# First down projection: eight of its 22 k tiles as seven products of block sums, and the position biases moved behind them

## The chip, the core and the metric

The kernel runs on one core of a Trainium2 chip, in one launch. Its time is the device time of the whole program in microseconds (us). TensorE (PE) multiplies, VectorE (DVE), ScalarE (ACT) and GpSimd (POOL) do the elementwise work, SyncE (SP) issues most DMAs. Each engine runs its own program in order and waits on semaphores where the program says so.

## The reference

Two transformer blocks follow each other on 256 tokens of 1024 features, all in float32. The first mixes tokens by forgetting attention and a gated delta rule, the second by neighbourhood attention and pooling; each ends in a feed-forward part. The change is in the feed-forward part of the first:

```python
hn = rmsnorm(h, norm_ffn[l])
up = causal_dwconv(jnp.einsum('bsd,df->bsf', hn, w_up[l]), ffn_conv_w[l])
u_gate, u_val = jnp.split(up, 2, axis=-1)
h = h + jnp.einsum('bsf,fd->bsd', jax.nn.silu(u_gate) * u_val, w_down[l])
```

`D_FF` is 2816, so the down projection multiplies a 256 x 2816 activation by a 2816 x 1024 weight: 22 k tiles of 128. The second block's feed-forward part has the same sizes, without the convolution. The biases are the second block's `rpb`, which neighbourhood attention adds to its scores.

## The kernel before

**Numbers.** Every float32 operand of a large product is split into a rounded part and a rest (`hi` and `lo`), and a product is three matmuls: hi x hi, lo x hi, hi x lo. The weights are split while the kernel runs.

**Steps.** All large products form one list of 258 steps (`HALVES`). A step is half a weight panel: 128 x 1024 numbers. SP loads panels into three raw buffers (`fetch`, L2590). For step n ACT rounds the raw half into `panel_hi` (`split`, L1238, copy at L1236), DVE subtracts to get `panel_lo` (`split`, L1740, L1754), PE multiplies (`gemm`, L710, matmuls at L652). Both have four buffers: ACT may write step n when PE has finished step n-4. In every engine's loop the pass for step n first splits step n+3 and then does what else is due at n, so that each elementwise job has a fixed place in its engine's queue, between two splits.

**The up projection** (steps 97 to 140): from its second pair of panels on, four steps make a gate and a value product of two feature tiles (a round, numbered j = 0 to 10). Per round DVE has four `panel_lo`, two `ffn_scaled` (bank times the row factor, L2097), two times four convolution taps (`ffn_taps`, L2109), one `ffn_silu` (L2115) and one `ffn_lo` (L2119, the lo half of the activation); POOL has one `ffn_mul` (L2517); ACT rounds the activation (`ffn_hi`, L1455).

**The first down projection** (steps 141 to 162): four banks, 2 x 512 columns by 2 x 128 tokens; `DOWN_ORDER` (L83) says which four k tiles and which columns each panel has. Each step is two k tiles by 512 columns for both token tiles, 12 matmuls of 512 columns. Beside it DVE adds the window mask to the position biases, one head in each of the passes 144 to 151 (`MASK_AT`, `mask_rpb`, L2122). The biases were loaded in the up projection, in the passes of `RPB_AT` (112, 116, 120, 124), the pooling bands and weights four and eight passes later.

**Its end.** `END["down", 0]` is 159 and `END["down", 1]` is 162. At such a step DVE adds the two banks of that column half to the residual `h` (`add_to_h`, L2029) and sums squares. PE, after the step that follows (160 and 163), waits for both adds of that half and transposes `h` (`turn_x`, L754, matmuls at L768) for the next products (`qk2`). POOL (`gained`, L2505), ACT and DVE multiply and sum further for the next norm.

**The second down projection** (steps 231 to 258) already does its first eight k tiles in seven products, by Winograd's form of Strassen's scheme: the activation is cut by k tiles and tokens, the weights by k tiles and column halves, `GROUPS` = 2 times. The four weight blocks of a group (128 x 1024 each) are loaded early (`block_raw`); each of the seven steps of a group splits a block or a sum of blocks, and DVE makes the four sums in place (`add_block`, L1731), each behind the split named in `ADDED_BEHIND`. Sums of the activation (`act2_sums` on POOL, L2526, then ACT's and DVE's halves, L1523 and L2199) are made for j = 0 to 3. Such a step has 6 matmuls of 512 columns. `GROUP_ORDER` puts a block step (named) and a plain step (None) in turn. The seven products go to seven banks, and DVE combines three of them with the others at the end (`block_sums`, L2055), before the last adds.

**Layout of time:** the DVE pass for step n is `split(n+3)` with its sum of blocks, then the adds and turns at an `END`, then `ffn_lo`, `ffn_silu`, `ffn_taps`, `ffn_scaled`, then a mask.

Of the kernel before, what the change touches and what calls it, by code (L numbers as in the profile page):

```python
# [17 lines left out]
F32 = mybir.dt.float32  # L18
# [52 lines left out]
for _name, _n in (("ident", P), ("upper", P), ("ones", 4), ("causal", P), ("decay_mask", P),  # L71
# [11 lines left out]
DOWN_ORDER = [(k, c) for k in range(0, KF - 6, HALF) for c in range(2)] + [(k, c) for c in range(2) for k in (16, 20)]  # L83
# [7 lines left out]
DOWN2_ORDER = [(8, 0), (8, 1), (12, 0), (12, 1), (16, 0), (20, 0), (16, 1), (20, 1)]  # L91
BLOCKS = ("b11", "b12", "b21", "b22")
GROUP_ORDER = [("b11", None, "b21", None, "b22", None, "t3", None, "t1", None, "t2", None, "t4", None),
               ("b11", None, "b21", None, "b22", None, "t3", None, "t1", "t2", None, "t4", None, None)]
ADDED_BEHIND = {"b11": "t1", "b21": "t3", "b22": "t2", "t3": "t4"}
BLOCK_BANK = {"b11": ("p1",), "b21": ("down2", 0, 0), "b22": ("down2", 1, 0), "t4": ("down2", 0, 1), "t1": ("p5",),
              "t2": ("p6",), "t3": ("p7",)}
SUM_3, SUM_1, SUM_2, SUM_4 = range(4)

# [5 lines left out]
def panels():  # L105
# [51 lines left out]
    for k, c in DOWN2_ORDER:  # L157
        add_wide(("down2", c), "act2", "w_down_2", k, min(HALF, KF - k), c * WIDE)
# [9 lines left out]
def with_blocks(halves):  # L168
    plain = [x for x in halves if PLAN[x[0]][0][0] != "down2"]
    down2 = iter(halves[len(plain):])  # L170
    return plain + [next(down2) if b is None else (None, g, b) for g, order in enumerate(GROUP_ORDER) for b in order] \
        + list(down2)
# [3 lines left out]
BLOCK_AT = {(g, b): n + 1 for n, (i, g, b) in enumerate(HALVES) if i is None}  # L176
# [5 lines left out]
          for i in range(len(PLAN))]  # L182
# [6 lines left out]
DOWN2_BANKS = [("down2", c, m) for c in range(2) for m in range(TT)] + [("p1",), ("p5",), ("p6",), ("p7",)]  # L189
TOUCHES = {key: [n + 1 for n, (i, _, b) in enumerate(HALVES)  # L190
                 if (BLOCK_BANK[b] == key if i is None else PLAN[i][0] == key[:2])] for key in DOWN2_BANKS}
for _c in range(2):
    END["down2", _c] = max(TOUCHES["down2", _c, m][-1] for m in range(TT))

# [20 lines left out]
BLOCKS_FROM = [END["up2", 1, 4], END["up2", 1, 6]]  # L215
# [6 lines left out]
RPB_AT = [END["up", 1, j] for j in (3, 4, 5, 6)]  # L222
MASK_AT = [END["up", 1, KF // 2 - 1] + 4 + i for i in range(HEADS)]
# [15 lines left out]
def build(nc, a, out, scratch_a, scratch_x, scratch_c):  # L239
    ctx = ExitStack()  # L240
    with ctx:
# [67 lines left out]
        gain_final = at("gain_final", [P, D], 19.5)  # L309
        sq2 = at("sq2", [P, TT, 2, PW], 23.5)  # L310
        block_at = [{"b11": 22, "b12": 22.5, "b21": 23, "b22": 23.5}, {"b11": 0, "b12": 0.5, "b21": 16.5, "b22": 21.5}]
        block_raw = [{b: at(f"block_{b}_{i}", [P, HALF * PW], block_at[i][b]) for b in BLOCKS} for i in range(2)]
        act_sums = [at(f"act_sums{i}", [P, 4, P], 21, skip=2048 * i) for i in range(2)]
        act_sums_hi = at("act_sums_hi", [P, 2 * GROUPS, 4, P], 18, F32R)
        act_sums_lo = at("act_sums_lo", [P, 2 * GROUPS, 4, P], 19.5, F32R)
# [188 lines left out]
        s_u_copied, s_block_sums = sem("p1_copied"), sem("block_sums")  # L504
# [45 lines left out]
        def down2_done(c, m):  # L550
            n = TOUCHES["down2", c, m][-1]
            return (s_half, n) if m or HALVES[n - 1][0] is None else filled(("down2", c, 0))
# [41 lines left out]
        def block_rows(g, b):  # L594
            r, c = int(b[1]) - 1, int(b[2]) - 1
            w = weights["w_down_2"][g * HALF * P:(g + 1) * HALF * P, wide(c)]
            return w.rearrange("(k r p) c -> r p k c", r=2, p=P)[r]
# [9 lines left out]
        def block_landed(g, b):  # L607
            return s_block[g][int(b[1]) - 1], 32

        def block_added(g, b):  # L610
            return s_block_add, len(ADDS) * g + ADDS.index(b) + 1
# [2152 lines left out]
```

## Time and profile before

| what | us |
|---|---|
| runs shown, median (lowest to highest) | 804.03 (802.47 to 804.63) |
| profiled execution, its own time | 802.98 |
| its span, first to last instruction | 801.5 |
| PE busy in the span | 795.6, 99% |
| DVE busy | 625.1, 78% |
| ACT busy | 457.2, 57% |
| POOL busy | 90.7, 11% |
| TensorE's granted clock | 1.000 of full speed throughout the span |

Some 1.5 us of the profiled execution lie outside its span. A timeline row gives the start, the busy time (of all its instructions, where it has several), the engine, the line, the operation, the tile written and the tiles read, their shapes and the count; in brackets the idle time ahead of it and what ended it. Two instructions of one engine may overlap by some 0.1 us, so the time from one start to the next is what an instruction costs its queue. Steps are counted along the `panel_lo` instructions of DVE, one a step.

### The profile page before, as it was taken

Reading aid. Unit: us, or ns where it says so; the run is one execution under the profiler, and the core shown is the slowest. Engines: PE = TensorE matmul, PEld = TensorE weight load, DVE = VectorE, ACT = ScalarE, POOL = GpSimd, SP = SyncE. Lnnn points to the kernel's source line nnn. Section 1 sums busy time; section 2 is a strip of 40 time slices with the busy share of each in tenths; the row PEclk is TensorE's granted clock in tenths of the full one; section 3 lists DMA queues with packets and bytes.
Section 4 is the critical chain, followed back from the end, with each engine's and each line's share of the span. In section 5 each row is a group of like instructions: output and inputs, shape, how many; then the busy total and the mean of one; then the engine's idle time right before and its main releaser. Section 6 shows DMA issues by size and latency. Waiting matters only on the chain. (4 is left out here: it accounts for less than half of the span.)

```text
span 801.5 us, 13178 instructions
## 1 busy us (share of the span) xinstructions
PE 795.6 (99%) x5164; PEld 696.8 (87%) x5164; DVE 625.1 (78%) x1035; ACT 457.2 (57%) x738; POOL 90.7 (11%) x77
## 2 busy tenths in 40 slices
PE   8999999999999999999999999999999999999998
PEld 6888888999898888899999998887778888888886
DVE  6888989785555766679999997486866898787977
ACT  6667677554535544456656563466665566555552
POOL 0001000010011302101101110011100333011100
PEclk9999999999999999999999999999999999999999
DMA  9654564557432555475687656464424666884331
GB/s 317 187 166 157 176 229 145 151 146 228 123 118 88 172 173 199 167 237 180 193 251 244 224 186 209 165 203 160 156 79 147 198 207 214 288 282 161 107 103 54
DMA packets 118125, 144.09 MB, mean 180 GB/s; under 512 B 11552, under 2 KB 86704, under 8 KB 117808
## 3 DMA queue, kind: packets, MB, share of 16 engines
q1 hardware_dynamic: 115616, 141.22, 54.7%
q10 hardware_dynamic: 2448, 2.03, 1.0%
q8 instruction: 41, 0.67, 0.3%
q14 instruction: 20, 0.16, 0.1%
HBM read 141.78 MB, written 1.46 MB: 179 GB/s over the span
## 5 line engine op out<-in xcount | busy, mean ns | idle before, releaser
L1754 DVE TENSOR_TENSOR panel_lo<-panel_raw,panel_hi 128x1024 fp32r<-128x1024 f32 x237 | 300.8, 1272 | 106.8 <-ACT panel_hi L1236 105.1
L652 PE MATMUL bank<-x_halves,panel_hi 128*128 128x256 f32 (+1 forms) x1536 | 367.0, 322 | 0.7 <-DVE x_halves L2222 0.7
L1236 ACT ACTIVATE panel_hi<-panel_raw 128x1024 fp32r<-128x1024 f32 (+1 forms) x239 | 252.2, 1057 | 152.9 <-PE bank L652 150.8
L652 PE MATMUL bank<-x_halves,panel_lo 128*128 128x256 f32 x1024 | 288.3, 282 | 0.0
L652 PEld LDWEIGHTS bank<-x_halves,panel_hi 128*128 128x128 f32 x1536 | 255.8, 190 | 23.3 <-issue 0.9
L652 PEld LDWEIGHTS bank<-x_halves,panel_lo 128*128 128x128 f32 x1024 | 195.0, 190 | 0.2
L652 PE MATMUL bank<-panel_hi,x_halves 128*128 128x512 f32 x384 | 122.1, 399 | 0.0
L652 PEld LDWEIGHTS bank<-panel_hi,x_halves 128*128 128x128 f32 x384 | 70.0, 188 | 14.4 <-DVE panel_lo L1754 0.6
L652 PE MATMUL bank<-panel_lo,x_halves 128*128 128x512 f32 x192 | 75.1, 391 | 0.0
L652 PE MATMUL bank<-panel_hi,act_hi 128*128 128x512 f32 x156 | 60.9, 390 | 0.2 <-DVE panel_lo L1754 0.2
L652 PE MATMUL bank<-panel_hi,act_lo 128*128 128x512 f32 x156 | 60.7, 389 | 0.0
L652 PE MATMUL bank<-panel_lo,act_hi 128*128 128x512 f32 x156 | 60.7, 389 | 0.0
L652 PEld LDWEIGHTS bank<-panel_lo,x_halves 128*128 128x128 f32 x192 | 36.0, 188 | 8.0
L2491 POOL TENSOR_TENSOR stats<-stats 128x2 f32<-128x2 f32 (+1 forms) x9 | 17.1, 1900 | 185.1 <-DVE stats L1768 104.0
L652 PEld LDWEIGHTS bank<-panel_hi,act_hi 128*128 128x128 f32 x156 | 29.3, 188 | 6.6 <-DVE panel_lo L1754 0.6
L652 PEld LDWEIGHTS bank<-panel_lo,act_hi 128*128 128x128 f32 x156 | 29.3, 188 | 6.1
L652 PEld LDWEIGHTS bank<-panel_hi,act_lo 128*128 128x128 f32 x156 | 29.3, 188 | 5.9
L1790 DVE SCALAR_TENSOR_TENSOR conv_acc<-conv_tmp,params,conv_acc 128x255 f32<-128x255 f32 (+2 forms) x72 | 30.5, 484 | 1.4 <-ACT conv_acc L1236 1.4
L2517 POOL TENSOR_TENSOR ff_tanh<-ff_tanh,ff_val 128x512 f32<-128x512 f32 x11 | 17.2, 1564 | 112.4 <-DVE ff_tanh L2115 112.4
L2496 POOL TENSOR_TENSOR key_bias<-key_bias,constants 128x128 f32<-128x128 f32 x16 | 8.9, 577 | 176.6 <-DMA key_bias<-gate_sums 176.6
L2524 POOL TENSOR_TENSOR f_tanh<-f_tanh,ff_val 128x512 f32<-128x512 f32 x11 | 15.2, 1385 | 94.0 <-DVE f_tanh L2191 94.0
L1748 DVE TENSOR_TENSOR panel_lo<-block_b,panel_hi 128x1024 fp32r<-128x1024 f32 x14 | 18.2, 1301 | 5.2 <-ACT panel_hi L1236 4.8
(312 smaller groups left out, 1017.1 us busy)
## 6 DMA issues: line engine op xcount, KB each, us to landing
panel_raw<-in_w_in SPq DMA_DIRECT2D x35, 1024.0 KB, 5.3
panel_raw<-in_w_up SPq DMA_DIRECT2D x30, 1024.0 KB, 5.4
panel_raw<-in_w_down SPq DMA_DIRECT2D x16, 1024.0 KB, 5.0
panel_raw<-in_w_gate SPq DMA_DIRECT2D x10, 1024.0 KB, 5.4
panel_raw<-in_w_out SPq DMA_DIRECT2D x8, 1024.0 KB, 5.0
panel_raw<-in_w_in SPq DMA_DIRECT2D x11, 512.0 KB, 4.7
panel_raw<-in_w_branch_fox SPq DMA_DIRECT2D x4, 1024.0 KB, 5.0
panel_raw<-in_w_branch_gdn SPq DMA_DIRECT2D x4, 1024.0 KB, 5.0
```

The source lines that it names most:

```text
L652: return e.matmul(o, l, r, start=start, stop=stop, skip_group_check=True)
L1236: return e.activation(o, i_, ACT.Copy, scale=scale)
L1748: e.tensor_tensor(wlo[w], block_raw[g][KEPT_IN[b]], whi[w].bitcast(F32), ALU.subtract) \
L1754: e.tensor_tensor(lo, raw_view(i, k0, kt), hi.bitcast(F32), ALU.subtract).then_inc(s_lo, 1)
L1790: e.scalar_tensor_tensor(acc[:, f, back:], tmp[:, f, 0:T - back], gconv(p, f, back), acc[:, f, back:], ALU.mult, ALU.add).then_inc(s_taps, 1)
L2491: return e.tensor_tensor(cols, cols, minus_half.broadcast_to([P, n]), ALU.pow)
L2496: i_ = e.tensor_tensor(key_bias[:, s], key_bias[:, s], C("causal"), ALU.add)
L2517: e.tensor_tensor(th, th, ff_acc[j % 2][1], ALU.mult).then_inc(s_f_mul, 1)
L2524: e.tensor_tensor(th, th, ff_acc[j % 2][1], ALU.mult).then_inc(s_g_mul, 1)
```

## The change

The first down projection gets the order of the second: 14 block steps and 14 plain ones (steps 141 to 168), with its own `GROUP_ORDER`, in which the second group ends `t1, t2, t4` and three plain steps. `END["down", 0]` becomes 165 and `END["down", 1]` 168; the last step of `p6` (`t2`) is 164. Its activation sums are made in the up projection for j = 0 to 3 (`sums`, `sums_hi`, `sums_lo`), its weight blocks are loaded there in every second pass from 116 to 130. The sums of the seven products are the same function for both projections, now right behind the split in DVE's pass, and `add_to_h` follows them. The bias loads move to passes 153 to 156, the bands to 165, the pooling weights to 166; the masks to passes 171, 173, 175, 177, 179, 181, 182 and 183.

```diff
-DOWN_ORDER = [(k, c) for k in range(0, KF - 6, HALF) for c in range(2)] + [(k, c) for c in range(2) for k in (16, 20)]
+DOWN_ORDER = [(8, 0), (8, 1), (12, 0), (12, 1), (16, 0), (20, 0), (16, 1), (20, 1)]
+GROUP_ORDER = {"down": [("b11", None, "b21", None, "b22", None, "t3", None, "t1", None, "t2", None, "t4", None),
+                        ("b11", None, "b21", None, "b22", None, "t3", None, "t1", "t2", "t4", None, None, None)],
...
 ADDED_BEHIND = {"b11": "t1", "b21": "t3", "b22": "t2", "t3": "t4"}
+BLOCK_BANK = {"b11": ("p1",), "b21": (0, 0), "b22": (1, 0), "t4": (0, 1), "t1": ("p5",), "t2": ("p6",), "t3": ("p7",)}
...
+BLOCKS_FROM = {"down": [END["up", 1, 4], END["up", 1, 6]], "down2": [END["up2", 1, 4], END["up2", 1, 6]]}
...
-RPB_AT = [END["up", 1, j] for j in (3, 4, 5, 6)]
-MASK_AT = [END["up", 1, KF // 2 - 1] + 4 + i for i in range(HEADS)]
+RPB_AT = [BLOCK_AT["down", 0, "t4"] + i for i in range(4)]
+MASK_AT = [END["down", 1] + i for i in (3, 5, 7, 9, 11, 13, 14, 15)]
...
+            def sums_hi(kind, j):
+                if j < 2 * GROUPS:
+                    e.wait_ge(s_sums, 3 * sums_of(kind, j) + 3)
+                    copy(act_sums_hi[kind][:, j], act_sums[kind][j % 2]).then_inc(s_sums_hi, 1)
...
             def ffn_hi(j):
                 e.wait_ge(s_f_mul, j + 1)
                 copy(acth[:, 2 * j:2 * j + 2, :], ff_tanh[j % 4]).then_inc(s_f_hi, 1)
+                sums_hi("down", j)
...
             def add_to_h(kind, c):
                 for m in range(TT):
-                    e.wait_ge(*product_of((kind, c), m))
+                    if kind in DOWNS:
+                        e.wait_ge(*down_done(kind, c, m))
+                        e.wait_ge(s_block_sums, BLOCK_SUMS)
...
+            def block_sums(kind, n):
+                p1, p5, p6, p7 = ((kind, p) for p in ("p1", "p5", "p6", "p7"))
+                if n == TOUCHES[p1][-1]:
                     e.wait_ge(s_half, n)
+                    add_to_rows(kind, 0, 0, bank_of(p1)).then_inc(s_block_sums, 1)
+                if n == TOUCHES[p6][-1]:
                     e.wait_ge(s_half, n)
+                    e.wait_ge(*emptied(p1))
+                    e.tensor_tensor(sum_u, bank_of(p6), sum_u, ALU.add).then_inc(empties(p6), 1)
+                    e.wait_ge(*emptied(p6))
+                    e.tensor_tensor(minus_w, bank_of(p5), sum_u, ALU.subtract).then_inc(s_block_sums, 1)
+                    e.tensor_tensor(sum_v, bank_of(p7), sum_u, ALU.add).then_inc(empties(p7), 1)
+                if n == TOUCHES[p6][-1] + 1:
+                    add_to_rows(kind, 1, 0, minus_w).then_inc(s_block_sums, 1)
+                    e.tensor_tensor(p5_less_v, bank_of(p5), sum_v, ALU.subtract).then_inc(empties(p5), 1)
+                    add_to_rows(kind, 0, 1, sum_v).then_inc(s_block_sums, 1)
+                    add_to_rows(kind, 1, 1, p5_less_v).then_inc(s_block_sums, 1)
...
+            def sums_lo(kind, j):
+                if j < 2 * GROUPS:
+                    e.wait_ge(s_sums_hi, sums_of(kind, j) + 1)
+                    e.tensor_tensor(act_sums_lo[kind][:, j], act_sums[kind][j % 2], act_sums_hi[kind][:, j].bitcast(F32),
+                                    ALU.subtract).then_inc(s_sums_lo, 1)
...
                 e.tensor_tensor(actl[:, 2 * j:2 * j + 2, :], ff_tanh[j % 4], acth[:, 2 * j:2 * j + 2, :].bitcast(F32),
                                 ALU.subtract).then_inc(s_f_lo, 1)
+                sums_lo("down", j)
...
             for n in range(1, STEPS + 1):
                 split(n + 3)
+                for kind in DOWNS:
+                    block_sums(kind, n)
...
                 if n - 1 in TAIL_AT:
                     ffn_mul(TAIL_AT[n - 1])
+                    sums("down", TAIL_AT[n - 1])
...
                 if n in RPB_AT:
                     r = RPB_AT.index(n)
-                    e.wait_ge(*product(("out", 1)))
+                    e.wait_ge(s_lo, BLOCK_AT["down", 0, "t4"])
                     e.dma_start(bias2[GRID * (r % 2):GRID * (r % 2) + GRID, :, r // 2, :],
                                 a["rpb_skew"][:, :, (3 - r) * GRID:(3 - r) * GRID + T]).then_inc(s_rpb, 16)
-                if n == RPB_AT[-1] + 4:
+                if n == BLOCK_AT["down", 1, "t4"]:
+                    e.wait_ge(s_lo, BLOCK_AT["down", 1, "t4"])
                     e.dma_start(band, a["bands"]).then_inc(s_band, 16)
```

`sums` on POOL is `act2_sums` for either projection: three instructions behind `ffn_mul`.

## Rows read from the trace of the kernel before

**Rows 1.** Windows: length, busy us (and count) of PE, PEld, DVE, ACT, POOL; clock; DMA
```profile
340.00:470.40 130.40, 130.40 (x1079) 129.89 (x1078) 121.74 (x179) 78.74 (x118) 16.60 (x11) 1.00 0.69 215
...
530.00:600.00 70.00, 70.00 (x357) 55.71 (x357) 50.49 (x111) 45.86 (x87) 7.19 (x4) 1.00 0.44 143
```
**Rows 2.** Timeline of ACT: up projection, first down projection, second down projection
```profile
384.29 1.06 ACT L1236 ACTIVATE panel_hi<-panel_raw 128x1024 fp32r<-128x1024 f32 x1 [0.49 <-PE bank L652]
...
395.81 1.06 ACT L1236 ACTIVATE panel_hi<-panel_raw 128x1024 fp32r<-128x1024 f32 x1 [0.49 <-PE bank L652]
...
487.03 1.06 ACT L1236 ACTIVATE panel_hi<-panel_raw 128x1024 fp32r<-128x1024 f32 x1 [1.66 <-PE bank L652]
489.75 1.06 ACT L1236 ACTIVATE panel_hi<-panel_raw 128x1024 fp32r<-128x1024 f32 x1 [1.66 <-PE bank L652]
...
787.92 1.06 ACT L1236 ACTIVATE panel_hi<-panel_raw 128x1024 fp32r<-128x1024 f32 x1 [0.30 <-PE bank L652]
789.28 1.06 ACT L1236 ACTIVATE panel_hi<-panel_raw 128x1024 fp32r<-128x1024 f32 x1 [0.30 <-PE bank L652]
```
**Rows 3.** Timeline of DVE in the up projection, rounds j = 1 to 4
```profile
377.24 1.21 DVE L1754 TENSOR_TENSOR panel_lo<-panel_raw,panel_hi 128x1024 fp32r<-128x1024 f32 x1
378.37 2.71 DVE L2109 SCALAR_TENSOR_TENSOR ff_gate<-ff_raw,params,ff_gate 128x255 f32<-128x255 f32 x4
...
387.78 0.69 DVE L2115 SCALAR_TENSOR_TENSOR ff_tanh<-ff_tanh,ff_gate 128x512 f32<-128x512 f32 x1
388.38 1.22 DVE L1754 TENSOR_TENSOR panel_lo<-panel_raw,panel_hi 128x1024 fp32r<-128x1024 f32 x1
...
399.78 2.28 DVE L1754 TENSOR_TENSOR panel_lo<-panel_raw,panel_hi 128x1024 fp32r<-128x1024 f32 x1 [0.17 <-ACT panel_hi L1236]
...
415.59 1.21 DVE L1754 TENSOR_TENSOR panel_lo<-panel_raw,panel_hi 128x1024 fp32r<-128x1024 f32 x1
```
**Rows 4.** Timeline of DVE in the second up projection, beside POOL's sums, j = 3
```profile
671.04 3.16 DVE L1754 TENSOR_TENSOR panel_lo<-panel_raw,panel_hi 128x1024 fp32r<-128x1024 f32 x2
674.13 0.95 DVE L2195 TENSOR_TENSOR act_lo<-f_tanh,act_hi 128x512 fp32r<-128x512 f32 x1
675.23 0.69 DVE L2199 TENSOR_TENSOR act_sums_lo<-act_sums,act_sums_hi 128x512 fp32r<-128x512 f32 x1 [0.15 <-ACT act_sums_hi L1236]
```
**Rows 5.** Matmuls by tile: duration min/median/max in ns, first and last start
```profile
L652 PE MATMUL bank<-panel_hi,act_hi x156: 387/389/499, 470.4 to 797.9; 128*128 128x512 f32 x156
```
**Rows 6.** Timeline of DVE before step 141, and one sum of blocks later
```profile
463.14 1.22 DVE L1754 TENSOR_TENSOR panel_lo<-panel_raw,panel_hi 128x1024 fp32r<-128x1024 f32 x1
464.29 1.66 DVE L2109 SCALAR_TENSOR_TENSOR ff_val<-ff_raw,params,ff_val 128x255 f32<-128x255 f32 x4
...
751.87 1.23 DVE L1738 TENSOR_TENSOR block_b<-block_b,block_b 128x1024 f32<-128x1024 f32 x1
```
**Rows 7.** Timeline of PE in the second down projection, start of step 238
```profile
754.89 0.50 PE L652 MATMUL bank<-panel_hi,act_hi 128*128 128x512 f32 x1 [0.20 <-DVE panel_lo L1754]
```
**Rows 8.** Timeline of DVE at the end of the second down projection
```profile
790.16 0.68 DVE L2063 TENSOR_TENSOR block_sum<-bank,block_sum 128x512 f32<-128x512 f32 x1
...
793.81 2.07 DVE L2050 SCALAR_TENSOR_TENSOR h<-block_sum,stats,h 128x512 f32<-128x512 f32 x3
795.99 2.15 DVE L2089 SCALAR_TENSOR_TENSOR h<-bank,stats,h 128x512 f32<-128x512 f32 x3
```
**Rows 9.** Timelines of DVE and PE at the end of the first down projection
```profile
521.91 1.28 DVE L2032 TENSOR_TENSOR h<-bank,h 128x512 f32<-128x512 f32 x2
...
531.64 1.28 DVE L2032 TENSOR_TENSOR h<-bank,h 128x512 f32<-128x512 f32 x2
...
524.86 1.03 PE L768 MATMUL bank<-constants,h 128*128 128x128 f32 x8
533.91 1.04 PE L768 MATMUL bank<-constants,h 128*128 128x128 f32 x8
```
**Rows 10.** DMA issues: tile and source, queue, count, KB each, median us to landing
```profile
block_b<-in_w_down SPq DMA_DIRECT2D x8, 512.0 KB, 7.2
```

More of the change, by code:

```diff
@@ L168, in with_blocks @@
 def with_blocks(halves):
[L169 to L172, printed above, removed]
+    out = []
+    for kind in DOWNS:
+        own = [x for x in halves if PLAN[x[0]][0][0] == kind]
+        out += halves[len([x for x in out if x[0] is not None]):halves.index(own[0])]
+        panel = iter(own)
+        out += [next(panel) if b is None else (None, (kind, g), b) for g, order in enumerate(GROUP_ORDER[kind]) for b in order]
+    return out
 HALVES = with_blocks(HALVES)
-BLOCK_AT = {(g, b): n + 1 for n, (i, g, b) in enumerate(HALVES) if i is None}
+BLOCK_AT = {(*g, b): n + 1 for n, (i, g, b) in enumerate(HALVES) if i is None}
 EARLY = (4, 5, 6)
@@ L665, in down2_bank, with down_first @@
                 return bank_of(key), n == TOUCHES[key][0], n == TOUCHES[key][-1]
[L667 to L669 removed]
+            def down_first(kind):
+                for key in BANKS_OF[kind]:
+                    bank_for("side" if key[1] in SUM_BANKS else "gemm", key)
             def block_product(n):
[L672 removed]
+                _, (kind, g), b = HALVES[n - 1]
                 hi, lo = (panel_view(w[(n - 1) % 4], "wide", 0, 2) for w in (whi, wlo))
[L674 removed]
+                o, first, last = down_bank(n, (kind, *BLOCK_BANK[b]))
                 e.wait_ge(s_lo, n)
@@ L697, in down2_product @@
                 for j in range(TT):
-                    o, first, last = down2_bank(n, ("down2", c, j))
+                    o, first, last = down_bank(n, (kind, c, j))
                     js = slice(j * P, (j + 1) * P)
@@ L711, in gemm @@
                 i, k0, kt = HALVES[n - 1]
-                if n == END["up2", 1, KF // 2 - 1] + 1:
-                    down2_first()
+                for up, kind in (("up", "down"), ("up2", "down2")):
+                    if n == END[up, 1, KF // 2 - 1] + 1:
+                        down_first(kind)
                 if i is None:
@@ L2618, in sync_program @@
                         fetch(i)
-                for g in range(GROUPS):
+                for kind, g in block_raw:
                     for at_, b in zip(range(0, 8, 2), ("b11", "b12", "b21", "b22")):
-                        if n == BLOCKS_FROM[g] + at_:
-                            e.wait_ge(*emptied(("out2", 1, 1)))
-                            e.dma_start(block_view(block_raw[g][b]), block_rows(g, b)).then_inc(block_landed(g, b)[0], 16)
+                        if n == BLOCKS_FROM[kind][g] + at_:
+                            if kind == "down":
+                                e.wait_ge(*product(("out", 1)))
+                            else:
+                                e.wait_ge(*emptied(("out2", 1, 1)))
+                            e.dma_start(block_view(block_raw[kind, g][b]), block_rows(kind, g, b)) \
+                                .then_inc(block_landed(kind, g, b)[0], 16)
                 if n == 3:
```

200 lines of the change are left out of this document (96 added, 104 removed), and 2 rows, old and new, of the table GROUP_ORDER.

## The prediction

> **What bounds the kernel now.** I read the windows by stage first, then the timelines of ACT and DVE in three places: a round of the up projection, the passage into each down projection, and the end of each. In the up projection PE is busy for all of 130.4 us and DVE for 121.74 of them [rows 1]: PE sets the pace, DVE is close behind. The pace is read from ACT, which in steady stretches starts a split when PE frees a buffer: a round of four steps is 11.52 us in the up projection (so 2.88 a step), a plain step of the first down projection is 2.72, and in the second down projection a block step is 1.36 [rows 2]. Twelve matmuls make 2.72, so one is 0.227 us. Step 141 begins at 470.4 [rows 5], and counting back 2.88 a step gives when PE needs each `panel_lo`.
>
> DVE's lead is the number to watch: how long before PE's start a `panel_lo` is done. Step 124 is needed at 470.4 - 17 x 2.88 = 421.44 and is done at 415.59 + 1.21 = 416.80: lead 4.64 [rows 3]. Step 141 is done at 464.36: lead 6.04 [rows 6]. Without idle time, DVE's round took 388.38 - 377.24 = 11.14 us, and only later does it stand idle for 0.17 in one [rows 3]. So DVE has 0.38 us a round to spare, and a lead of some 5 us that hides anything that is late once.
>
> **PE's work.** Before: 22 steps of 2.72, 59.84 us. After: 14 of 1.36 and 14 of 2.72, 57.12 us. Gain **2.72**, which is all that the change can bring, since PE has no idle time elsewhere to lose.
>
> **The activation sums in the up projection (rounds 0 to 3).** DVE gets one more subtraction of 128x512, 0.60 us of its queue (387.78 to 388.38) [rows 3]. POOL gets three instructions behind its product, and DVE waits while POOL works: a split of 1.21 takes 2.28 beside POOL's product [rows 3]. What three such sums cost DVE is seen in the second up projection: two splits in 3.16 instead of 2 x 1.14, so 0.88, and an `act_lo` of 0.95 instead of 0.69, so 0.26 [rows 4]. That is 0.60 + 1.14 = 1.74 a round, against 0.38 to spare. There DVE had idle time beside it, here it has none. In four rounds DVE falls 7.0 us back in work. The lead of 4.64 at step 124 (worked out with the 0.38 already spent) and 0.17 of idle time take up 4.8. PE waits for the rest: **2.2**. Bounds: 0, if the lead absorbs all; 10.4, if each of POOL's three costs what its product does, 1.07 (4 x (0.60 + 3.21) - 4.8). I take the row of the same instructions. ACT waits for POOL's sums in its own queue ahead of its copy, with `ff_gate` copies and the next split behind it; its queue is busy for 78.74 of 130.4 [rows 1], so I count that at nothing.
>
> **The passage from up to down, steps 141 to 148.** After step 124 the lead is 0. Four rounds give back 4 x 0.38 = 1.5 by step 140. Step 141 stands better in its round than 124 does, by up to 6.04 - 4.64 = 1.4; I take 1.1, as some of the 1.4 is recovery. Lead at 141: 2.6, so its split begins 2.6 + 1.2 = 3.8 before PE's step 141. From there to the end of the split of step 148 DVE's queue holds, in order of program: 8 splits at 1.13 (9.1), 4 sums of blocks at 1.23 (4.9) [rows 6], 3 groups of taps at 1.57 (1.66 less the overlap, 4.7), 2 each of `ffn_scaled`, `ffn_silu`, `ffn_lo` at 0.60 (3.6), and twice 1.07 for POOL's last two products (2.1). That is 24.4, ending 20.6 after PE began step 141. PE, in four block and three plain steps, wants step 148 at 4 x 1.36 + 3 x 2.72 = 13.6. PE waits **7.0**. With the old lead (7.2 instead of 3.8) it would be 3.6. The lowest bound is the same passage in the second down projection, where PE stands idle for 0.20 at step 238 [rows 7]; its rounds have no taps. The highest is a lead of nothing at 141: 9.6. I stay with 7.0, the queue counted out. From step 149 on a pair of steps lasts 4.08 on PE and asks two splits and at most one sum of blocks of DVE, 3.5: no wait, and the masks are gone from there.
>
> **The end of column half 0.** The last step of `p6` is 164. Behind it DVE has in one queue: three sums, a split, four more sums and adds, then the two `add_to_h`; PE's transposes after step 166 wait for these. The second down projection ran this very queue: ACT is released by the `p6` step at 789.28 [rows 2], the sums start at 790.16, the last adds at 795.99, two of three are done by 797.39 [rows 8]: 8.1 us after the release. Five of these have no row factor now (0.62 instead of 0.70): 7.8. PE spends 1.36 + 2.72 = 4.08 on steps 165 and 166, then stands: 3.7, and up to 0.3 more as PE's step ends before ACT sees it. I take **3.9**. Queued behind the transposes are steps 167 and 168; nothing else can run on PE. Before, the adds were done at 523.19 and PE came at 524.86 [rows 9]: no wait. Bounds: 0, if the queue took half as long; 4.5.
>
> **Column half 1.** From the first adds to the second took 523.19 to 532.92, 9.73 us (norm sums, turns, splits, POOL's product in between) [rows 9]. PE comes back after 1.03 + 3 x 2.72 = 9.19. Before, PE was later than the adds by the 1.7 us above; now both start together: **0.5**. Bounds 0 and 1.
>
> **Moves.** The masks, 8 of 0.60, go to a stretch in which DVE is busy for 50.49 of 70 us [rows 1], one in a pass, mostly ahead of an idle place: 0, at most 4.8. The biases and bands, issued by SP behind waits on splits that SP's fetches of the same passes need anyway, are in time for step 171: 0. The block loads (512 KB, 7.2 us to landing) [rows 10] share the up projection's DMA with panels, which are fetched three panels ahead: 0, at most 2.
>
> **The sum:** -2.72 + 2.2 + 7.0 + 3.9 + 0.5 = **+10.9** on the profiled execution's 802.98: 813.9. That execution lies 1.05 below the median of the runs; on the median it is 814.9. I put down **814.4**.
>
> **Rivals.**
> 1. *The lead hides POOL's sums* (DVE's instructions slip between POOL's, or ACT's waits cover them): no wait in the up projection and the old lead at 141. -2.72 + 3.6 + 4.4 = +5.3: about 809. For it: the second up projection bears the same sums without a wait of PE. Against it: DVE's rounds there are lighter. 0.20.
> 2. *Only the end waits*: the passage goes as in the second down projection, 0.2 [rows 7]. -2.72 + 0.2 + 4.4 = +1.9: 805.6. Against it: 4.7 us of taps that the other passage doesn't have. 0.06.
> 3. *The clock falls in the pause.* In all rows PE works without a break and its granted clock is 1.00 [rows 1]; a pause of 3.9 us occurs in none. If the clock came back at the lower of its two levels, 1.2 GHz, for steps 167 and 168, their 5.44 us would double: +16.3 at most, 820. 0.08. The Trainium skill ("TensorE: Matmul & The Clock Gate", section "What's actually happening") holds that TensorE drops to half rate when it has been idle and earns full rate by work; no run here shows it yet. By that page alone the sum would be the one of this rival.
> 4. *The other sign: the sums of the products do not hold the turn.* If DVE's queue behind step 164 took 4.1 us or less instead of 7.8, and the passage cost under 0.2, PE's gain would stand: -2.72 + 0.2, 800.5. It decides at the point where the `add_to_h` of half 0 ends before step 166 does. Against it: the same queue, measured [rows 8]. 0.05.
> 5. *More than counted*: masks in the attention's stretch and DMA at their bounds, +6.8 at most, some 818. 0.06.
>
> My forecast has 0.55. A measurement of this kernel tells no change from a change of some 0.3%, 2.4 us. Rival 4 is faster: 0.05. Rival 2 is no change: 0.06. The others are slower: 0.89. The range 805 to 819 leaves out rival 4, some of rival 2 and the upper half of rival 3.
>
> **What would show it.** In the profile after: idle time of PE ahead of L652, released by DVE's `panel_lo`, some 2 us between steps 112 and 124 and some 7 us in steps 142 to 148; an idle stretch of some 4 us ahead of the transposes of `h` that follow step 166, released by `h` of `add_to_h`; DVE without idle time through rounds 0 to 3; PE's busy time less by the 12 matmuls. Wrong would be: no idle PE ahead of step 120 (the lead held), none ahead of the transposes (the queue is shorter than I count), or PE waiting on DMA.

## The result and the profile after

The changed kernel takes **814.76 us** (median of 4 runs, 813.74 to 815.01) against 803.96 for the kernel before: ratio 1.0136, 95% interval 1.012 to 1.0152. The profiled execution took 815.01 (before 802.98), its span is 813.6 (before 801.5): 12.1 more. Forecast were 814.4 and +10.9.

Windows of the kernel after, columns as in [rows 1]: the up projection, steps 141 to 147, a stretch within that passage, two within the turn of `h`, and the turn into the attention.
```profile
340.00:470.30 130.30, 130.30 (x1077) 129.56 (x1076) 125.16 (x181) 78.02 (x117) 28.07 (x22) 1.00 0.66 219
470.30:491.10 20.80, 16.06 (x63) 12.02 (x61) 20.53 (x26) 10.92 (x15) 4.42 (x2) 0.92 0.20 75
481.20:484.10 2.90, 2.90 (x8) 2.29 (x7) 2.81 (x4) 1.42 (x2) 0.00 (x0) 0.50 0.86 312
...
532.40:539.00 6.60, 5.56 (x17) 4.74 (x18) 6.16 (x10) 4.35 (x10) 2.81 (x1) 0.50 0.79 284
533.40:538.90 5.50, 5.46 (x17) 4.71 (x18) 5.09 (x8) 3.63 (x10) 2.81 (x1) 0.50 0.76 276
530.00:600.00 70.00, 65.42 (x315) 52.83 (x316) 56.28 (x112) 43.06 (x79) 10.93 (x5) 0.95 0.51 174
```
In the up projection PE shows no idle time (two late starts that hide behind this follow below). In steps 141 to 147 it is busy for 16.06 us of 20.80 while DVE works for 20.53: there DVE sets the pace. Twice the granted clock is 0.50, the lower of the two levels (1.2 GHz); before it was 1.00 throughout.

PE's timeline of the kernel after. These are the first instruction of steps 141, 142, 144 and 148, a matmul of the slow stretch and its successor, the transposes of both halves of `h` (against 524.86 and 533.91 in [rows 9]) and the turn of q and k:
```profile
470.29 0.40 PE L669 MATMUL bank<-panel_hi,act_hi 128*128 128x512 f32 x1
...
472.16 0.50 PE L669 MATMUL bank<-panel_hi,act_hi 128*128 128x512 f32 x1 [0.32 <-DVE panel_lo L1779]
...
480.05 0.50 PE L669 MATMUL bank<-panel_hi,act_hi 128*128 128x512 f32 x1 [3.51 <-DVE panel_lo L1779]
...
482.00 0.63 PE L669 MATMUL bank<-panel_hi,act_hi 128*128 128x512 f32 x1
482.43 0.63 PE L669 MATMUL bank<-panel_hi,act_lo 128*128 128x512 f32 x1
...
491.10 0.50 PE L669 MATMUL bank<-panel_hi,act_hi 128*128 128x512 f32 x1 [0.91 <-DVE panel_lo L1779]
...
533.44 1.94 PE L786 MATMUL bank<-constants,h 128*128 128x128 f32 x8 [3.93 <-DVE h L2061]
...
545.21 1.03 PE L786 MATMUL bank<-constants,h 128*128 128x128 f32 x8
...
566.66 1.06 PE L1081 MATMUL bank<-constants,qk 128*128 128x128 f32 x8 [1.14 <-DVE qk L2176]
```
Starts are 0.43 apart in the slow stretch instead of 0.227. Step 148 starts 491.10 - 470.29 = 20.81 after step 141; PE's work in between is 13.6 at full clock. So 7.2 us are lost there.

DVE's timeline in the up projection of the kernel after: the same split in three rounds running (its place in [rows 3] is 377.24 and 388.38), and the splits of steps 120 and 124 (the latter there at 415.59):
```profile
377.93 1.21 DVE L1779 TENSOR_TENSOR panel_lo<-panel_raw,panel_hi 128x1024 fp32r<-128x1024 f32 x1
...
390.56 1.21 DVE L1779 TENSOR_TENSOR panel_lo<-panel_raw,panel_hi 128x1024 fp32r<-128x1024 f32 x1
...
403.19 1.21 DVE L1779 TENSOR_TENSOR panel_lo<-panel_raw,panel_hi 128x1024 fp32r<-128x1024 f32 x1
...
408.24 1.21 DVE L1779 TENSOR_TENSOR panel_lo<-panel_raw,panel_hi 128x1024 fp32r<-128x1024 f32 x1
...
419.97 1.21 DVE L1779 TENSOR_TENSOR panel_lo<-panel_raw,panel_hi 128x1024 fp32r<-128x1024 f32 x1
```
A round takes DVE 12.63 us where it took 11.14. The `panel_lo` of step 124 is done at 421.18. Counted back, PE wants it at 470.29 - 17 x 2.88 = 421.33, a lead of 0.15 out of 4.64. But PE's starts show that nothing was left of it:
```profile
409.23 0.28 PE L669 MATMUL bank<-x_halves,panel_lo 128*128 128x256 f32 x1
409.50 0.51 PE L669 MATMUL bank<-x_halves,panel_hi 128*128 128x256 f32 x2
...
421.00 0.28 PE L669 MATMUL bank<-x_halves,panel_lo 128*128 128x256 f32 x1
421.24 0.50 PE L669 MATMUL bank<-x_halves,panel_hi 128*128 128x256 f32 x2
```
Steps 120 and 124 start at 409.50 and 421.24, 0.05 and 0.06 behind the end of their `panel_lo` (409.45, 421.18). Here matmuls of 128x256 start 0.12 apart and each is recorded with 0.28, so a pause that short shows in the starts alone and not as idle time.

**Where 12.1 us went.** I compare PE's timeline by stations: the transposes of half 1 of the "ffn" turn (345.53 before, 344.93 after), those of both halves of `h`, and those of the first qk turn. The first station comes 0.60 earlier. From there to the transposes of half 0 it is 188.51 instead of 179.33 (+9.18); to half 1 11.77 instead of 9.05 (+2.72); to the qk turn 21.45 instead of 20.32 (+1.13); to the end 0.33 less. The 9.18 are -2.72 of PE's work, 0.46 up to step 141 (the late starts of steps 120 and 124), 7.2 in the passage, 3.9 of idle time ahead of the transposes, and 0.3 that I don't place.

### The profile page after: what moved, and what is told of

It is laid out like the page before. It is cut to its first block and busy times, and to the rows that moved or that the text cites. A ratio compares the mean times of both kernels' runs of the same rounds, so it can differ in the third digit from the quotient of the medians.

```text
span 813.6 us, 13230 instructions
## 1 busy us (share of the span) xinstructions
PE 798.2 (98%) x5152; PEld 697.3 (86%) x5152; DVE 653.6 (80%) x1061; ACT 464.4 (57%) x749; POOL 104.1 (13%) x89
## 3 DMA queue, kind: packets, MB, share of 16 engines
q10 hardware_dynamic: 2448, 2.03, 0.9%
## 5 line engine op out<-in xcount | busy, mean ns | idle before, releaser
L1779 DVE TENSOR_TENSOR panel_lo<-panel_raw,panel_hi 128x1024 fp32r<-128x1024 f32 x229 | 284.6, 1245 | 88.7 <-ACT panel_hi L1254 86.5
L1254 ACT ACTIVATE panel_hi<-panel_raw 128x1024 fp32r<-128x1024 f32 (+1 forms) x231 | 242.5, 1053 | 102.1 <-PE bank L669 100.6
L669 PEld LDWEIGHTS bank<-panel_hi,x_halves 128*128 128x128 f32 x384 | 70.0, 188 | 14.4 <-DVE panel_lo L1779 0.6
L669 PE MATMUL bank<-panel_hi,act_hi 128*128 128x512 f32 x136 | 54.9, 404 | 4.7 <-DVE panel_lo L1779 4.7
L669 PE MATMUL bank<-panel_hi,act_lo 128*128 128x512 f32 x136 | 54.5, 401 | 0.0
L669 PE MATMUL bank<-panel_lo,act_hi 128*128 128x512 f32 x136 | 54.3, 399 | 0.0
L1773 DVE TENSOR_TENSOR panel_lo<-down_block_b,panel_hi 128x1024 fp32r<-128x1024 f32 x28 | 36.4, 1299 | 7.8 <-ACT panel_hi L1254 6.8
L2554 POOL TENSOR_TENSOR ff_tanh<-ff_tanh,ff_val 128x512 f32<-128x512 f32 x11 | 23.6, 2141 | 104.6 <-DVE ff_tanh L2153 104.6
L1254 ACT ACTIVATE panel_hi<-down_block_b 128x1024 fp32r<-128x1024 f32 x28 | 29.6, 1057 | 11.2 <-PE bank L669 11.2
L669 PEld LDWEIGHTS bank<-panel_hi,act_lo 128*128 128x128 f32 x136 | 26.3, 193 | 5.4
L2147 DVE SCALAR_TENSOR_TENSOR ff_gate<-ff_raw,params,ff_gate 128x255 f32<-128x255 f32 (+1 forms) x44 | 30.7, 757 | 0.0
```

Of the source, the lines that this page charges most:

```text
L669: return e.matmul(o, l, r, start=start, stop=stop, skip_group_check=True)
L1254: return e.activation(o, i_, ACT.Copy, scale=scale)
L1773: e.tensor_tensor(wlo[w], block_raw[group][KEPT_IN[b]], whi[w].bitcast(F32), ALU.subtract) \
L1779: e.tensor_tensor(lo, raw_view(i, k0, kt), hi.bitcast(F32), ALU.subtract).then_inc(s_lo, 1)
L2147: e.scalar_tensor_tensor(acc[:, c, back:], raw_[:, c, 0:T - back], fconv(s, j, c, back), acc[:, c, back:], ALU.mult, ALU.add).then_inc(s_f ...
L2554: e.tensor_tensor(th, th, ff_acc[j % 2][1], ALU.mult).then_inc(s_f_mul, 1)
```

## The experiments

Each ratio is to the kernel before, run on the same chip; the kernel after is 1.0136. The theory: DVE's queue sets the loss, at two places where it lies badly against PE's steps. The main rival: DVE has too much work everywhere, so that no order helps.

The kernel before took 803.96 beside the kernel after and 802.5 beside the experiments. So a ratio set against 1.0136 shows some 1.4 us too little gain, and an expectation below that works with gains of 1.9 and 2.0 has them too small. The traces don't depend on this: the time from the first station (the "ffn" turn) to the end of the span leaves out the start, which differs by up to 1.8 us between executions. Up to step 141 it agrees within 0.03 in the kernel after and ten of the experiments. One profiled execution each:

| kernel | ratio | station to end, against the kernel after |
|---|---|---|
| before | 1 | -12.7 |
| plain steps first | 1.0112 | -4.4 |
| sums earlier | 1.0111 | -4.0 |
| PE busy at the turn | 1.0145 | -1.5 |
| PE busy in the passage | 1.0147 | -1.1 |
| POOL's first sum twice | 1.0165 | +0.5 |
| masks moved | 1.0158 | +0.6 |
| both orders | 1.0061 | -7.8 |
| both orders, two moves | 1.0033 | -10.3 |
| `add_to_h` first | 1.002 | -11.0 |
| short sums of blocks | 1.0103 | -4.0 |
| short sums of blocks, `add_to_h` first | 0.9993 | -13.2 |
| less work on DVE | 0.998 | -14.4 |

**Plain steps first.** In group 0:
```
-    "down": [("b11", None, "b21", None, "b22", None, "t3", None, "t1", None, "t2", None, "t4", None),
+    "down": [(None, None, None, "b11", None, "b21", None, "b22", None, "t3", None, "t1", "t2", "t4"),
```


> Only the order of column group 0 of the first down projection is changed: three plain steps first, then b11, b21, b22, t3 with plain steps between, t1, t2 and t4 last. Same instructions, same count. Theory (DVE's queue is piled up in steps 141 to 148, as three sums of blocks and the last taps meet four short block steps): counted as in the prediction, eight splits 9.1, two sums of blocks 2.5, taps, ffn and POOL's last products 10.4, less the 4.0 by which the split of step 141 begins ahead, end 18.0 after PE began step 141, and PE, with five plain steps and two short ones, wants step 148 at 16.3. So the lost time between steps 141 and 148, 6.9 us in the kernel after (waits 5.3 and 1.6 at the lower clock), falls to 1.7, no fall of the clock there, and the time is about 809.5. Rival (DVE has more work than PE in the whole group, so the wait only moves behind step 148): waits of 4 us or more in steps 149 to 160, and 813 to 815.

Ratio 1.0112 (1.0095 to 1.0129). PE's waits of that run:
```profile
481.69 0.50 PE L669 MATMUL bank<-panel_hi,act_hi 128*128 128x512 f32 x1 [1.58 <-DVE panel_lo L1779]
486.80 0.50 PE L669 MATMUL bank<-panel_hi,act_hi 128*128 128x512 f32 x1 [0.71 <-DVE panel_lo L1779]
530.36 1.53 PE L786 MATMUL bank<-constants,h 128*128 128x128 f32 x8 [3.93 <-DVE h L2061]
```
In the passage 2.3 of idle time is left of 4.7, without a fall of the clock. A wait of 0.8 is new in group 1; DVE stands idle for 1.61 there, for ACT, behind its add of p1 to `h`. From the station to the transposes of half 0 it is 185.33 instead of 188.51: 3.2 us won, of 5.2 expected (and 810.7 us, not 809.5). The order matters, and part of the wait moved, as the rival had it.

**The sums earlier.** In group 1, so that `t2` is step 162 instead of 164:
```
-    ("b11", None, "b21", None, "b22", None, "t3", None, "t1", "t2", "t4", None, None, None)],
+    ("b11", None, "b21", "b22", None, "t3", "t1", "t2", None, "t4", None, None, None, None)],
```


> Only the order of column group 1 is changed: t2, the last product of the sums, comes at step 162 instead of 164, so that PE has 9.5 us of steps from there to its transposes instead of 4.1. Theory (the transposes wait for DVE's queue of 7.8 us behind p6, and the clock falls in that wait): no wait ahead of the transposes after step 166, granted clock 1.00 there; 3.9 and 2.5 are won back, and 0.5 to 1.5 is lost where two blocks now stand side by side (b21 and b22, two splits and two sums are 4.7 on DVE against 2.7 on PE) and at the end of half 1: 809 to 810. Rival (DVE's whole work between t2 and the second column half sets the end, so the wait moves to the transposes of half 1): a wait of 3 us or more there, 812 to 814.

Ratio 1.0111 (1.0096 to 1.0126). The turns of `h` and of q and k ("issue" stands where the profile names no releaser):
```profile
530.82 1.06 PE L786 MATMUL bank<-constants,h 128*128 128x128 f32 x8 [0.56 <-issue]
540.56 1.06 PE L786 MATMUL bank<-constants,h 128*128 128x128 f32 x8 [0.47 <-issue]
...
562.68 1.07 PE L1081 MATMUL bank<-constants,qk 128*128 128x128 f32 x8 [1.14 <-DVE qk L2176]
```
The wait at the turn falls from 3.93 to 0.56 (DVE's last add still ends only at 530.72), the fall of the clock there is gone, and half 1 follows after 9.74 instead of 11.77. The turn of q and k then follows after 22.12 instead of 21.45: 0.7 is given back. A wait of 0.43 is new at step 159, behind the two blocks side by side. 811.3 us is above the 809 to 810 expected.

**PE kept busy in the pauses.** Matmuls whose result nobody reads, ahead of the wait for `h`, and in another kernel 13 of them ahead of the wait of step 144:
```
...
+    for _ in range(16):
+        mm(bank_of(("down", "p1")), acth[:, 0, 0:P], acth[:, 0:2, :])
     for m in range(TT):
         e.wait_ge(*emptied((kind, c, m)))
```


> 16 matmuls of 128x512 (3.6 us) are added ahead of PE's wait for h after step 166, into a bank that is free, read by nobody; nothing else is changed. Theory (the lower clock after the wait costs 2.5 us by itself, beside the wait of 3.9): the transposes begin where they did, granted clock 1.00 in steps 167 and 168, the transposes take 1.03 instead of 1.59; 0.5 of it goes to a wait ahead of the transposes of half 1, so 2.0 won: 812.8. Rival (the slow stretch is covered, as DVE sets the time of half 1 anyway): the clock is 1.00, but PE then waits about 2.5 ahead of the transposes of half 1, and the time is 814.5 to 815.

> 13 matmuls of 128x512 (2.95 us) are added ahead of PE's wait for panel_lo of step 144, into a bank that is free, read by nobody; nothing else is changed. Theory (DVE's queue sets when step 148 can start, so the 1.6 us that the lower clock costs in steps 144 to 147 are time that PE would have waited in any case): granted clock 1.00 through the passage, PE's wait ahead of step 148 grows from 0.9 to about 2.5, step 148 starts when it did, and the ratio to the kernel before stays at 1.0136 within 0.1%. Rival (the slow clock is a loss of its own): the wait ahead of 148 stays about 0.9, and 1.6 us are won, ratio 1.0116.

Ratios 1.0145 (1.013 to 1.016) and 1.0147 (1.0132 to 1.0162): by these no gain can be told from none in either. The traces show more. At the turn (first kernel) the transposes stood 9.74 apart instead of 11.77, so the slow clock had cost 2.0 there, but the qk turn came 22.13 after half 1 instead of 21.45: 1.35 of it stays won, between the theory's 2.0 and the rival's nothing. In the passage (window of steps 141 to 147, and the starts of steps 144, 146 and 148 in the second kernel):
```profile
470.92:491.74 20.82, 17.69 (x75) 13.28 (x73) 20.55 (x26) 10.93 (x15) 4.41 (x2) 1.00 0.23 76
```
```profile
480.69 0.50 PE L670 MATMUL bank<-panel_hi,act_hi 128*128 128x512 f32 x1 [0.55 <-DVE panel_lo L1785]
486.46 0.50 PE L670 MATMUL bank<-panel_hi,act_hi 128*128 128x512 f32 x1 [1.35 <-DVE panel_lo L1785]
...
491.74 0.50 PE L670 MATMUL bank<-panel_hi,act_hi 128*128 128x512 f32 x1 [0.91 <-DVE panel_lo L1785]
```
At clock 1.00 the stretch lasts 20.82, with the clock at 0.50 in it 20.81: there the slow clock costs nothing, it fills time that PE would have waited for DVE. Only the place was off: the wait came back ahead of step 146, not 148. What this kernel won, it won at the turn, where half 1 followed after 10.72.

**POOL's first sum twice** in rounds 0 to 3, each on a semaphore of its own:
```
+    e.tensor_tensor(s_[:, SUM_3:SUM_1 + 1, :], x_[:, 0:2, :], x_[:, 1:4:2, :], ALU.subtract).then_inc(s_twice, 1)
+    e.wait_ge(s_twice, j + 1)
     e.tensor_tensor(s_[:, SUM_3:SUM_1 + 1, :], x_[:, 0:2, :], x_[:, 1:4:2, :], ALU.subtract).then_inc(s_sums, 1)
```


> POOL makes the first of its three sums of activations twice (0.8 us more per round) in rounds 0 to 3 of the first up projection; nothing else is changed. Theory (POOL's sums eat DVE's lead, and at step 124 of the kernel after 0.15 us of it was left): DVE's round rose from 11.14 to 12.64 there, 0.60 of it the subtraction and 0.90 POOL's three sums of 1.85 in all, so 0.8 more on POOL cost DVE 0.4 a round; the lead is used up by round 2 or 3, PE waits 1.0 to 1.6 us for panel_lo between steps 112 and 124, and the time rises by as much. Rival (DVE's instructions slip between POOL's, the lead was lost to the subtraction alone): no wait of PE there and the lead at 124 still above 0.

Ratio 1.0165 (1.0144 to 1.0185). PE's waits from 400 to 430, and the start that follows this wait:
```profile
PE bank L669 <- DVE panel_lo L1779: 1.1, 1, 1.1
```
```profile
411.72 0.51 PE L669 MATMUL bank<-x_halves,panel_hi 128*128 128x256 f32 x2 [1.15 <-DVE panel_lo L1779]
```
PE waits 1.15 ahead of step 120, and 0.16 ahead of step 116, between steps 112 and 124 as forecast for the kernel after. Up to step 141 it is 1.57 longer than there (1.0 to 1.6 expected), so the rival falls: 0.8 more on POOL goes straight into PE's time once the lead is used up. To the end only 0.5 of it is left, as half 1 followed half 0 after 10.69 instead of 11.77.

**The masks moved.** Three each directly ahead of the two normalisings of q and k, two between:
```
-MASK_AT = [END["down", 1] + i for i in (3, 5, 7, 9, 11, 13, 14, 15)]
+MASK_AT = [END["down", 1] + i for i in (7, 7, 7, 9, 9, 11, 11, 11)]
```


> The eight masks are moved on DVE: three each directly ahead of the two places where DVE waits for POOL's power of the means of q and k, two between them; nothing else is changed. Theory (two masks between the splits ahead of the means put POOL's power, the normalised q and k and so PE's turn of q and k off by 1.2 to 1.4): PE's wait of 1.1 ahead of the turn of q and k, by DVE's qk, is gone or under 0.2, and the time is 813.5. Rival (the masks fill idle time, and PE's wait comes from the late end of the down projection): the wait stays, 814.5 to 815.

Ratio 1.0158 (1.0143 to 1.0174). The first wait went, and one of 1.40 came at the second qk turn, behind the three masks put there. How the first went shows that I had the mechanism wrong. DVE ahead of the first normalising and POOL's power, in the kernel after:
```profile
561.27 1.23 DVE L1779 TENSOR_TENSOR panel_lo<-panel_raw,panel_hi 128x1024 fp32r<-128x1024 f32 x1
...
561.44 3.82 POOL L2528 TENSOR_TENSOR stats<-stats 128x16 f32<-128x16 f32 x1 [8.50 <-DVE stats L2171]
```
and with the masks moved:
```profile
561.44 1.23 DVE L1779 TENSOR_TENSOR panel_lo<-panel_raw,panel_hi 128x1024 fp32r<-128x1024 f32 x1 [0.16 <-ACT panel_hi L1254]
...
561.36 2.89 POOL L2528 TENSOR_TENSOR stats<-stats 128x16 f32<-128x16 f32 x1 [8.23 <-DVE stats L2171]
```
The means are ready at nearly the same time in both (0.08 apart). But in the kernel after two masks had filled the idle time ahead of them (0.85 with the masks moved), so DVE's next split no longer waited 0.16 for ACT, and it started ahead of POOL's power: that took 0.93 longer, and q and k with it.

**Both orders, then two moves.** Group 0 is now `b11`, five plain steps, `b21`, plain, `b22`, `t1`, `t3`, plain, `t2`, `t4`; group 1 as above. In a second kernel also:
```
-MASK_AT = [END["down", 1] + i for i in (3, 5, 7, 9, 11, 13, 14, 15)]
+MASK_AT = [END["down", 1] + i for i in (7, 7, 7, 9, 11, 13, 14, 15)]   # run behind qk_normalise
-    if n == TOUCHES[p1][-1]:                  # DVE: p1 to h; ACT's copy of p1 three steps later
-        e.wait_ge(s_half, n)
+    if n == TOUCHES[p1][-1] + 2:
+        e.wait_ge(s_half, TOUCHES[p1][-1])
```


> Both groups of the first down projection are reordered: group 0 is b11, five plain steps, b21, plain, b22, t1, t3, plain, t2, t4; group 1 as in the run before with t2 at step 162. Same instructions, same count. Theory (DVE's queue is long enough in sum and only lies badly): waits of PE in steps 142 to 148 of 0.5 to 1.0 instead of 5.3 and 1.6, ahead of the turn of half 0 under 1.0 instead of 3.9 and 2.5, half 1 later by 0.7, the turn of q and k later by 1.1: -2.72 + 0.8 + 0.8 + 0.7 + 1.1 = +0.7, ratio 1.001 (1.000 to 1.003). Rival (the two single reorderings won 1.9 and 2.0 us and more than that is not there, since DVE's work per step is above PE's all through): ratio 1.0085 or more.

> The reordering of both groups, and with it two moves: DVE's add of p1 to h and ACT's copy of p1 stand two and three steps later (ACT's copy held up its next splits while DVE stood behind PE's step), and three masks stand behind the normalising of the first q and k, where DVE is idle for 3.2 us, instead of ahead of its means. Theory: no wait of PE in group 1 of the down projection, POOL's power for the first q and k takes 2.9 instead of 3.8 as DVE's next split does not stand ahead of it, PE's wait of 1.1 ahead of the turn of q and k goes: ratio 0.999 (0.997 to 1.001). Rival (the wait ahead of the turn of q and k comes from the late end of the down projection and not from the masks): that wait stays, ratio as without the two moves.

Ratios 1.0061 (1.0044 to 1.0077) and 1.0033 (1.002 to 1.0046). Both fall short of the theory (1.001, 0.999) and beyond the rivals: the order alone wins back 7.8 of 12.7 us. In the first kernel the largest wait was one that the theory did not have, ahead of step 159:
```profile
510.61 0.50 PE L669 MATMUL bank<-panel_hi,act_hi 128*128 128x512 f32 x1 [1.66 <-DVE panel_lo L1779]
```
In the second it is gone, the wait of the qk turn is gone too, and POOL's power takes 2.90, so the rival on the masks falls. What is left are waits of 1.26 in steps 142 to 144, 1.16 and 0.48 ahead of the two turns of `h`, and 0.53 behind half 1.

**`add_to_h` ahead of the split of its pass**, on top of that:
```
 for n in range(1, STEPS + 1):
+    for c in range(2):
+        if n == END["down", c]:
+            add_to_h("down", c)
     split(n + 3)
```


> The run with both orders and the moved masks, and besides DVE's add_to_h of both column halves stands ahead of the split of its pass instead of behind it. Theory (the split of 1.13 ahead of it is not wanted by PE until after the turn): waits ahead of the two turns of h fall from 1.16 and 0.48 (and 0.39 more in each gap) to 0.3 together; the wait of 0.53 at the step after half 1 grows by up to 0.7, since DVE's work stays the same: 0.6 to 1.6 won, ratio to the kernel before 1.0015 to 1.0025. Rival (DVE's queue as a whole is the bound, the wait only changes its place): ratio 1.003.

Ratio 1.002 (1.0012 to 1.0029), as the theory had it: both waits ahead of the turns go, and the one behind half 1 grows from 0.53 to 0.87. This wait without and with the move:
```profile
545.32 0.73 PE L669 MATMUL bank<-panel_hi,x_halves 128*128 128x512 f32 x2 [0.53 <-DVE panel_lo L1779]
```
```profile
544.77 0.50 PE L669 MATMUL bank<-panel_hi,x_halves 128*128 128x512 f32 x1 [0.87 <-DVE panel_lo L1779]
```

**Less work in DVE's sums of blocks**, in the kernel after and in the kernel with `add_to_h` first. Both leave out 960 of the 1024 columns of each sum, so their products are not the reference's:
```
+    part = slice(0, 64 if kind == "down" else HALF * PW)
+    e.tensor_tensor(to[:, part], to[:, part], block_raw[kind, g][OTHER[t_]][:, part], ALU.add).then_inc(s_block_add, 1)
-    e.tensor_tensor(to, to, block_raw[kind, g][OTHER[t_]], ALU.add).then_inc(s_block_add, 1)
```


> The kernel after, but the eight sums of blocks of the first down projection add only 64 of the 1024 columns (the rest of the sums is left out); all waits stand. Theory (DVE's queue sets the passage, and its sums of blocks of 1.23 are part of it): with two to three sums before the step that binds, 2.1 to 3.3 us of the lost time between steps 141 and 148 go (6.9 in the kernel after), the wait of 3.9 ahead of the turn of half 0 stays, as its queue holds none of them: ratio 1.0095 to 1.011. Rival (the last rounds' taps and the lag from the up projection alone set it): passage as in the kernel after, ratio 1.0136.

> The run with add_to_h first, and the same sums of blocks on 64 of 1024 columns (the rest left out). Theory (what is left of the loss is DVE's work, 9 us of it in these eight sums): waits ahead of the turns go, 0.8 to 1.5 remain in steps 142 to 146 and at half 1, and PE's 2.72 shows at last: ratio 0.998 to 1.000. Rival (DVE is no bound any more once the order is right): ratio as in the run with add_to_h first.

Ratios 1.0103 (1.0089 to 1.0117) and 0.9993 (0.9984 to 1.0003). PE's waits in the first of them:
```profile
PE bank L786 <- DVE h L2062: 3.9, 1, 3.9
PE bank L669 <- DVE panel_lo L1780: 2.5, 2, 2.1
```
The wait in the passage falls from 4.7 to 2.5 and the one at the turn stays at 3.9: DVE's sums of blocks are part of the first and not of the second. In the second kernel waits of 1.4 are left, and 2.2 us are won on top of `add_to_h` first: DVE's work still bounds it once the order is right.

**Work taken off DVE.** On top of `add_to_h` first, with all sums whole: `ffn_mul` on DVE, POOL's gained product of half 0 on DVE, and one split in DVE's wait for POOL's power.
```
     ffn_silu(TAIL_AT[n - 1])
+    ffn_mul(TAIL_AT[n - 1])          # DVE; taken out of POOL's program
...
+    split(n + 4)                     # n = END["down", 1] + 1, and not again in the next pass
     e.wait_ge(s_rms, 3)
```


> The run with add_to_h first, and three further moves, all for DVE's queue: ffn_mul of the first up projection runs on DVE instead of POOL (a split of 1.21 took 2.28 beside POOL's product, so the product cost DVE 1.07 a round, and done by DVE itself it is one 128x512 instruction of 0.60); POOL's gained product of half 0, beside which a 0.69 square of DVE took 2.89, runs on DVE as well (1.28); and the split of step 173 stands in the first of the two places where DVE waits 0.8 for POOL's power. Theory (what is left of the loss in the run with add_to_h first is DVE's work: 0.48 + 1.12 + 0.21 in the passage, 0.65 between the turns, 1.03 behind half 1): the lead at step 141 grows by about 0.47 a round, the waits in the passage go, and 2.0 to 3.3 us are won: ratio to the kernel before 0.998 to 0.9995. Rival (the loss that is left comes from waits that DVE's work doesn't set): ratio 1.002 as in the run before.

800.87 us, ratio **0.998** (0.9971 to 0.9989): faster than both kernels. PE's waits from 340 to 600, and the two turns of `h`:
```profile
PE bank L1081 <- DVE qk L2182: 1.4, 1, 1.4
```
```profile
522.33 1.06 PE L786 MATMUL bank<-constants,h 128*128 128x128 f32 x8
531.43 1.04 PE L786 MATMUL bank<-constants,h 128*128 128x128 f32 x8
```
No wait is left between the up projection and half 1, and half 1 follows after 9.10 (9.05 before). The wait of the qk turn is back: POOL's power again started behind a split. DVE's round with `ffn_mul` became 0.3 shorter, not 0.47: 12.33 with POOL's sums, 10.82 without. The three moves were not tried one by one, nor on the kernel before, where PE has no idle time for them to win. But they act at different places: 2.95 of the gain over `add_to_h` first lies ahead of the turn of half 0, where only `ffn_mul` was changed, 0.5 between the turns, and behind half 1 the wait of 0.87 is gone and the one of 1.4 has come.

## Why the prediction was right, step by step

- **PE's work, -2.72.** It shows nearly in full only where the waits are gone: the last kernel reaches the transposes of half 0 176.82 after the station, 2.51 less than before.
- **Up projection, 2.2: too dear, 0.46.** The step "POOL gets three instructions behind its product, 1.14 a round" priced the sums too high. By step 124 DVE had fallen back 419.97 - 415.59 + 0.60 = 4.98. It had also taken up the idle time that was there before: 0.17, and 0.27 in the next round (row below), which the prediction did not read. That is 5.42 instead of 7.0. A round rose by 1.49 at most, not 1.74, so POOL's sums cost DVE at most 0.9, not 1.14. The prediction's sign of being wrong, no idle PE ahead of step 120, came true in the profile. Rival 1 (the lead hides the sums) was near on this wait but not on the lead, of which nothing was left at step 124.
```profile
411.30 2.19 DVE L1754 TENSOR_TENSOR panel_lo<-panel_raw,panel_hi 128x1024 fp32r<-128x1024 f32 x1 [0.27 <-ACT panel_hi L1236]
```
- **Passage, 7.0: right, 7.2.** The queue counted out by instruction, with a lead of 2.6 (measured 2.8), gave it: 24.4 counted, 24.8 measured from the start of step 141's split to the end of step 148's. The lead came out right because it starts from nothing at step 124, with a wait of 2.2 or of 0.46. In form it was 4.7 of idle time, the rest a slow clock and matmuls restarting; the run with PE kept busy (20.82 against 20.81) shows that DVE sets the total.
- **End of half 0, 3.9: right, 3.93.** The second down projection ran the same queue, and its rows gave the price: 7.8 forecast from ACT's release to the last add, 7.8 measured.
- **Half 1, 0.5: off by the clock.** At full clock it was 0.69 (9.74 against 9.05); 2.03 more came from the clock.
- **Clock (rival 3): came in part.** The granted clock fell to 0.50 in the passage, behind an idle time of 3.51, and at the turn, within one of 3.93; it did not fall around 2.11, 1.66 or 1.58 in other kernels. The Trainium skill ("TensorE: Matmul & The Clock Gate", section "What's actually happening") has it that an idle TensorE drops to half rate, and here the trace agrees. But the price was 2.0, not the 5.4 by which this rival had steps 167 and 168 longer (its 16.3 is the whole sum), and with the clock kept up 0.7 of it was given back at the qk turn.
- **Masks at 0: wrong, 1.1.** They are hidden, as I counted; what I left out is that they moved DVE's split ahead of POOL's power.
- **Rivals 2 and 4** fall with the passage of 7.2 and the turn of 3.93. Of rival 5 only the masks' 1.1 came; no wait of PE from the up projection to the qk turn is for a DMA.

The total is thus near for two reasons. The two large terms, 7.0 and 3.9, were right in size and mechanism. And, by luck, an up projection 1.7 us too dear stood against the clock and POOL's power, 3 us that I put at nothing. From the first station to the end the loss was 12.7, 1.8 more than the forecast of 10.9.

## What to carry to other kernels

Where a second engine keeps pace with the first, price an edit by the second one's queue at the place where it lies, instruction by instruction, from the lead that is left there. A saving on the engine that works without a break is worth only what its suppliers can follow: here 2.72 us of matmuls were bought with eight sums of 1.23 on DVE, among others, and showed only once the order of steps and a few moves had given DVE the time. A kernel part that already runs the same queue elsewhere is the best price list. And where executions differ by more than the effect, the time between two stations of the traces shows it.

## What the runs showed of the hardware

- **Who starts first decides.** POOL's first power of 128x16 behind the means of q and k took 2.89 or 2.90 in the kernels in which DVE's split came behind it (before, and four of those above) and 3.80 to 3.84 where the split was already running (the kernel after and eight others). The Trainium skill ("SBUF — State Buffer", section "Who interferes with whom") says that a DVE instruction with two inputs in SBUF contends with a GpSimd instruction that reads SBUF, that the lock is exclusive, and that the order in which they are issued decides who is blocked. With DVE first this agrees. With POOL first it depends on POOL's instruction: in the kernel before, a split that began 0.09 behind POOL's product took 2.28 instead of 1.21 (399.78 in [rows 3]), but the split that began 0.08 behind POOL's power took 1.23, as alone. What makes the difference was not tried. The product of that row:
```profile
399.69 1.30 POOL L2517 TENSOR_TENSOR ff_tanh<-ff_tanh,ff_val 128x512 f32<-128x512 f32 x1 [8.93 <-DVE ff_tanh L2115]
```
- **A slow clock can be free.** In the passage 20.81 with the clock at 0.50 for part of it, and 20.82 at 1.00, each time with DVE busy almost throughout.
- **A full PE can wait unseen.** Matmuls of 128x256 start 0.12 apart and are recorded with 0.28, so the 0.46 that PE lost at steps 120 and 124 is no idle time in any window; the starts, or two stations, show it.
- **The same pause, two prices.** An idle time of 3.93 ahead of the transposes put half 1 11.77 behind half 0 in the kernel after, but 10.72 in the kernel with the passage kept busy. The traces show the clock low for longer in the first, from ahead of the transposes (533.44) on: in the second it stood at 1.00 when they began (534.09) and fell later. Why it fell earlier in one than in the other was not tried. Windows of the second, beside 532.40 to 539.00 of the kernel after:
```profile
534.00:535.30 1.30, 1.21 (x10) 1.20 (x11) 0.87 (x3) 1.10 (x3) 1.18 (x1) 1.00 1.09 366
535.50:538.80 3.30, 3.30 (x9) 2.64 (x8) 3.30 (x4) 1.81 (x6) 1.45 (x1) 0.50 0.80 300
```
